# Turning the softmax maps with a diagonal of reciprocals in place of the identity

## What is computed

```python
def attend(q, k, v):                       # layer 0: 16 heads, 4 key/value heads
    s = jnp.einsum("bkgqd,bkld->bkgql", q, k).astype(jnp.float32) * scale
    p = _softmax32(s).astype(v.dtype)
    return jnp.einsum("bkgql,bkld->bkgqd", p, v)
...
def attend(q1, q2, k, v):                  # layer 1: 8 heads, two maps each
    s1 = jnp.einsum("bhqd,bhld->bhql", q1, k[0]).astype(jnp.float32) * scale
    s2 = jnp.einsum("bhqd,bhld->bhql", q2, k[1]).astype(jnp.float32) * scale
    p = _softmax32(s1) - lam * _softmax32(s2)
    return jnp.einsum("bhql,bhle->bhqe", p.astype(v.dtype), v)
```

## Time and profile before

| | |
|---|---|
| median of three runs | 2618.81 us (2612.16, 2618.81, 2623.81) |
| the profiled execution | 2617.47 us, span 2615.7 us, mean granted TensorE clock 0.976 |
| TensorE matmuls, weight loads | busy 94%, 75% |
| VectorE, ScalarE, GpSimd | busy 53%, 43%, 13% |
| costliest group | the dense products of L1510 |
| loop of layer 0 | scores from 147.6 us, last transposes at 238.3 us |
| loop of layer 1 | scores from 865.8 us, last transposes at 954.8 us |
| loop of layer 3 | scores from 2300.9 us, last transposes at 2365.2 us |

### The profile page before, as it was taken

One profiled execution on the slowest core, in us unless ns is written; L12 is line 12 of the kernel. 1 busy time (PEld: TensorE's weight loads), 2 busy tenths in 40 slices (PEclk: granted clock), 3 DMA queues, 4 the chain that ended last, 5 costly groups with the idle time before them and its releaser, 6 DMA issues. The chain is left out here.

```text
span 2615.7 us, 38016 instructions
## 1 busy us (share of the span) xinstructions
PE 2447.6 (94%) x15310; PEld 1966.2 (75%) x15310; DVE 1399.0 (53%) x2162; ACT 1134.9 (43%) x1936; POOL 333.4 (13%) x270
## 2 busy tenths in 40 slices
PE   6989899999999889999999997889999999978997
PEld 3655777778789558777788887777777788947997
DVE  2475565443443766555534335756545435476874
ACT  3365543333342565333323443445333324366663
POOL 0000311111100003111102002322111012002111
PEclk8999999999999999999999998999999999998998
DMA  7611356653232002656532320014656434603663
GB/s 243 212 38 59 112 169 182 185 179 103 78 99 86 25 23 66 186 178 185 175 97 83 104 81 26 2 49 126 187 178 185 136 99 88 160 21 93 183 184 98
DMA packets 500851, 311.32 MB, mean 119 GB/s; under 512 B 24178, under 2 KB 499618, under 8 KB 500548
## 3 DMA queue, kind: packets, MB, share of 16 engines
q1 hardware_dynamic: 498048, 307.39, 39.9%
q10 hardware_dynamic: 2628, 1.50, 0.2%
HBM read 307.80 MB, written 1.05 MB: 118 GB/s over the span
## 5 line engine op out<-in xcount | busy, mean ns | idle before, releaser
L1510 PE MATMUL bank<-h_hi,slab_hi 128*128 128x512 f32 (+1 forms) x2416 | 857.9, 355 | 37.9 <-DVE slab_lo L946 26.0
L1510 PE MATMUL bank<-h_lo,slab_hi 128*128 128x512 f32 (+1 forms) x2416 | 835.8, 346 | 0.0
L1510 PE MATMUL bank<-h_hi,slab_lo 128*128 128x512 f32 (+1 forms) x2416 | 835.3, 346 | 0.0
L946 DVE TENSOR_TENSOR slab_lo<-slab_raw,slab_hi 128x1024 fp32r<-128x1024 f32 (+1 forms) x388 | 538.8, 1390 | 542.6 <-ACT slab_hi L521 541.5
L521 ACT ACTIVATE slab_hi<-slab_raw 128x1024 fp32r<-128x1024 f32 (+1 forms) x388 | 401.5, 1036 | 524.1 <-PE bank L1510 271.2
L1510 PEld LDWEIGHTS bank<-h_hi,slab_hi 128*128 128x128 f32 x2416 | 464.0, 192 | 149.2 <-issue 89.6
L1510 PEld LDWEIGHTS bank<-h_hi,slab_lo 128*128 128x128 f32 x2416 | 464.4, 192 | 55.7
L1510 PEld LDWEIGHTS bank<-h_lo,slab_hi 128*128 128x128 f32 x2416 | 464.5, 192 | 50.0 <-issue 0.5
L915 ACT ACTIVATE conv<-bank,prm 128x512 f32<-128x512 f32 (+1 forms) x176 | 127.3, 723 | 362.7 <-PE bank L1510 362.4
L1510 PE MATMUL bank<-g_hi,slab_hi 128*128 128x512 f32 (+1 forms) x770 | 269.3, 350 | 2.1 <-ACT res_t L572 2.1
L1510 PE MATMUL bank<-g_hi,slab_lo 128*128 128x512 f32 (+1 forms) x770 | 267.2, 347 | 0.0
(11 more groups left out here) (210 smaller groups left out, 2770.1 us busy)
## 6 DMA issues: line engine op xcount, KB each, us to landing
slab_raw<-in_mod_w SPq DMA_DIRECT2D x192, 512.0 KB, 4.6
slab_raw<-in_ffn_w_up SPq DMA_DIRECT2D x176, 512.0 KB, 4.5
slab_raw<-in_ffn_w_down SPq DMA_DIRECT2D x64, 512.0 KB, 4.1
slab_raw<-in_ffn_w_down SPq DMA_DIRECT2D x32, 384.0 KB, 3.6
slab_raw<-in_b_w_qkv SPq DMA_DIRECT2D x24, 512.0 KB, 3.7
slab_raw<-in_c_w_in SPq DMA_DIRECT2D x24, 512.0 KB, 3.7
slab_raw<-in_d_w_qkv SPq DMA_DIRECT2D x24, 512.0 KB, 6.7
slab_raw<-in_a_w_qkv SPq DMA_DIRECT2D x12, 512.0 KB, 5.3
```

What stands on the lines that cost most here:

```text
L946: nc.vector.tensor_tensor(wlo[slot][:, 0:w], raw[of][:, 0:w], whi[slot][:, 0:w].bitcast(f32), ALU.subtract).then_inc(s_lo, 1)
L1510: ins = mm(out, l, r, start=first and n == 0, stop=last and n == 2)
```

## The change

The exponentials stay as they are. The reciprocal of the row sum goes into a diagonal matrix, the identity times the reciprocal as a scalar of each partition, and the block is turned by an ordinary product with this diagonal, which turns and scales at once. In layer 1 the sum of the two maps is formed on the unscaled exponentials: p1 plus p2 times the ratio (second reciprocal times -lambda times the first sum), and the diagonal then holds the first reciprocal. The diagonals have five buffers at the top of the on-chip memory, so the writing of a diagonal waits until the unit five before has been turned. `p_ready` is now raised by the diagonal.

```diff
+        diag_at = [nc.sbuf_usable_end // 64 * 64 - MAPS * 4 * P]
+        diag = [place(f"diag{s}", [P, P], at=diag_at) for s in range(MAPS)]
...
                         for m in range(maps):
                             ins = nc.vector.reciprocal(stat[:, 4 + m, w:w + 1], stat[:, 2 + m, w:w + 1])
                         link(ins)
-                        r1 = stat[:, 4, w:w + 1]
-                        if maps == 1:
-                            nc.vector.tensor_scalar(p1[w % MAPS][:, 0:nk], p1[w % MAPS][:, 0:nk], r1, None,
-                                                    ALU.mult).then_inc(S["p_ready"], 1)
-                        else:
-                            nc.vector.tensor_scalar(p1[w % MAPS][:, 0:nk], p1[w % MAPS][:, 0:nk], r1, None, ALU.mult)
-                            link(nc.vector.tensor_tensor(stat[:, 5, w:w + 1], stat[:, 5, w:w + 1], small[:, 13:14],
-                                                         ALU.mult))
-                            nc.vector.scalar_tensor_tensor(p1[w % MAPS][:, 0:nk], p2[w % MAPS][:, 0:nk],
-                                                           stat[:, 5, w:w + 1], p1[w % MAPS][:, 0:nk],
-                                                           ALU.mult, ALU.add).then_inc(S["p_ready"], 1)
+                        if maps == 2:
+                            ratio = stat[:, 5, w:w + 1]
+                            link(nc.vector.scalar_tensor_tensor(ratio, ratio, small[:, 13:14], stat[:, 2, w:w + 1],
+                                                                ALU.mult, ALU.mult))
+                            nc.vector.scalar_tensor_tensor(p1[w % MAPS][:, 0:nk], p2[w % MAPS][:, 0:nk], ratio,
+                                                           p1[w % MAPS][:, 0:nk], ALU.mult, ALU.add)
+                        if w >= MAPS:
+                            dve.wait_ge(S["p_turned"], w - MAPS + 1)
+                        nc.vector.tensor_scalar(diag[w % MAPS][:], ident, stat[:, 4, w:w + 1], None, ALU.mult).then_inc(S["p_ready"], 1)
...
                         for kt in range(2 if U[w][1] == 0 else 4):
-                            ins = nc.tensor.transpose(pb[:, kt * P:kt * P + P], p1[w % MAPS][:, kt * P:kt * P + P], ident)
+                            ins = mm(pb[:, kt * P:kt * P + P], p1[w % MAPS][:, kt * P:kt * P + P], diag[w % MAPS][:],
+                                     start=True, stop=True)
                         ins.then_inc(S["p_turned"], 1)
```

More of the change, by code:

```diff
@@ L269, in build_program @@
         window = place("window", [P, GRID_W], at=at)
+        assert at[0] <= diag_at[0] - 4 * P * MAPS
         at = [arena + 4 * (16 * T + 4 * D)]
```

## The result

The changed kernel takes 2632.2 us (median of 20 runs, 2626.7 to 2634.4) against 2617.6 for the kernel before in the same comparison: a ratio of 1.0053, 95% interval 1.0046 to 1.0059. By the medians that is 14.6 us, or 0.5%, slower, on the border of what was called measurable. The forecast was 2628.2 with a range of 2614 to 2639: the direction and the range held, and 4 us were missing.

A forecast was written before the change was run, and what follows sets the result against it. Prediction: TensorE becomes the bound in layers 0 and 3, while layer 1 hides its added work. Layer 0 +8.7, layer 1 -1.6 and layer 3 +3.6 give +10.7 on 2617.5, so 2628.2 us; range 2614 to 2639.

The forecast's parts named there:

- The price of a block: Turning on TensorE: an ordinary f32 product takes 0.225 us a block instead of 0.11, +0.115, over 416 blocks.
- an equal price: Turning on TensorE: a product with a diagonal costs what the transpose costs; 2613.6 us; chance 0.12.
- the rival of four transposes: Turning on TensorE: a product costs four transposes, 0.44 against 0.11 us, +0.33 a block; 2693 us; chance 0.02.
- TensorE's sum: Layer 0: TensorE's work in one period without waits, 9.50 us, plus 2.96 added, 12.46, becomes the bound.
- the ring: Layer 0: the period's loop over VectorE and ScalarE, 11.36 us before, grows only by about 0.13.
- The cover: Layer 1: TensorE's 2.49 us idle a period hides its added 1.5 us.
- the rival of a lost cover: Layer 1: if the cover is gone, 1.5 us a period, 10 us; partly gone (+2) within rival (2), chance 0.26.
- the prediction's mixed ring: Layer 3: loop through VectorE and TensorE, one group of transposes +0.53, one scaling -0.20, giving 7.93 us a period.
- the fourth rival: Full clock in layer 3's tail and in 3.4 us at 875 in layer 1: 2627 us; chance 0.10.
- VectorE's 19 us: Narrower scaling saves VectorE 8.6, 4.3 and 6.4 us in layers 0, 1, 3: the most the change could bring.
- rival (1): Product costs what the transpose costs, leaving only VectorE's gain in layers 1 and 3: -3.9, 2613.6 us; chance 0.12.
- Scores apart: Layer 0: two short scores stay apart, +0.64 us a period, +4.5; with layer 1's cover partly gone 2634.7; chance 0.26.

The follow-up runs named there:

- the kernel with the identity product: Kernel before, scaling kept on VectorE, every block turned by an ordinary product with the identity instead of the transpose: 2633.0 against 2619.1 us, ratio 1.0057.
- the partial kernels: Kernel before, identity product only for some layer 0 units: short 2625.1 us, long 2622.8, units 4 and 5 2623.9, units 7, 0 and 1 2622.7.
- the VectorE half: Changed kernel with diagonals written and awaited, but blocks turned by the transpose with the identity, leaving reciprocal scaling out of the result: ratio 0.9998 against the kernel before.
- the kernel with long units alone: Kernel before, identity product instead of the transpose only for layer 0's long units, 16 blocks a period: 2622.8 us, period 11.87 us.
- the filled wait: Kernel before with four never-read 128x128 by 128x512 products put into TensorE's wait ahead of layer 0's loop: 2618.2 us, one run.

## Why the prediction was right or wrong

- **The price of a block: right.** 0.225 us forecast from the earlier trace rows; eight blocks start to start take 1.98 in the changed kernel (208.44 to 210.42 with the step to the next product), 0.25 a block with entering the set included. The rivals of an equal price and of four transposes are out by this pace, and the kernel with the identity product has the same 832 instructions and the same period. (In the rival of four transposes the 5 us for layer 1 are too few: by its own prices 12 x 0.33 + 0.1, less the 2.49 idle, is 1.6 a period and 11 us in all. Nothing hangs on it.)
- **Layer 0's period: right number, half the reason.** 12.46 forecast, 12.50 measured. TensorE's sum was right to 0.04 (12.42 of work by starts), and the kernel with the value products moved shows it at work. The step that failed is the bracket "the ring grows only by about 0.13": the ring passes through three sets of blocks on TensorE, which the first paragraph on layer 0 had itself named as what the score stands behind. Added up from the partial kernels it grows by 0.98 + 0.14 = 1.12, to 12.48, and the wait of 0.08 that is left on TensorE in the changed kernel fits a ring that is just the longer of the two. The two bounds happen to meet, so that the forecast of this period came out is in part luck; had the change touched only the short units, the same reasoning would have said "nothing" for 0.61 a period.
- **Layer 0 in all: +8.7 forecast, +12.1 in the pair of traces.** This is the mis-sized term. Seven periods at +1.10 were charged; there are six regular intervals (+1.14 each, 6.9 us), and the seventh is the tail, which was charged by itself (+0.95 forecast, +0.9 measured). The start was put at nothing, without a reason, and costs 4.4 in this pair of traces: 2.1 for the added passes at full clock, where I can't say for each whom it delays, and the rest for half clock, which stretches eight pairs from 1.09 to 2.00 us. The 6.8 us of half clock stood in the trace of before, at 145.0; the prediction named the clock only in layer 3's tail and at 875 in layer 1.
- **Layer 1: −1.6 forecast, about −0.1 measured** over eleven kernels (above). The cover held: 1.5 us a period of added TensorE work cost nothing (11.93 and 11.94 with the scaling kept), so the rival of a lost cover is out. Failed: seven intervals where there are four regular ones; the ratio kept at 0.153 where it takes 0.220; and the interval behind the regular ones, +0.8 where a tail of +0.3 was counted.
- **Layer 3: +3.6 forecast, +2.1 measured.** The period is near the forecast (7.98, measured 8.05, with 7.96 of work on TensorE), but TensorE's sum alone doesn't hold it: the kernel with the identity product has the same work and 8.11. With the 0.05 that the VectorE half took off in place of 0.20, the prediction's mixed ring would be 7.60 + 0.53 - 0.05 = 8.08 (an estimate), so here too the ring is at least level; no run separates the two in the changed kernel. And there are five regular intervals, not seven (5 x 0.44 = 2.2). The tail was to cost +0.9 with its half clock kept; it is 0.2 shorter, because the half clock of the earlier trace rows is gone. That was the fourth rival's point, and it came true in this place only. Over more traces the layer costs a little more than in this pair: 70.0 to 71.4, mean 70.6, in the seven kernels that leave it as it was, and 72.4 to 73.5, mean 73.1, in the three that hold the whole change in it.
- **VectorE's 19 us: right for layer 0, too high in the others.** "Nothing" in layer 0 held. By rival (1) the VectorE half alone was worth 3.9 us in layers 1 and 3; with the transposes kept it gives a ratio of 0.9998, and 3.9 lies just outside that interval.
- **Scores apart** (second rival): in the changed kernel they go out nearly together, with 0.08 of wait where the rival charged 0.64 a period. Its price, 2634.7, is nearer to the result than the forecast (2.5 us off, against 4.0), but its mechanism is nearly absent. In the kernel with long units alone it does show: four pairs in 1.09 instead of 0.63, a wait of 0.45.
- **Chances.** Slower by over 0.5% had 0.34; the result is 0.53% (0.46 to 0.59), on the line. With the start at its price, and the other layers at what they measured, the sum would have been 10.7 + 3.4 (layer 0) + 1.5 (layer 1) − 1.5 (layer 3) = 14.1, and the chances about even.

The clock in the tail of layer 3, in the kernel before with the filled wait, over the same stretch as the earlier trace rows, where TensorE still does transposes (it stays at 1.00 up to the layer's end):

```profile
2360.25:2363.66 3.41, 1.90 (x16) 1.34 (x18) 2.30 (x7) 2.27 (x7) 0.00 (x0) 1.00 0.00 0
```

So transposes alone don't settle it. Of nine kernels that turn layer 3 by transposes, eight have 3.4 us at half clock between 62 and 64 us into this layer, and this one has not; of five that turn it by products none has. The end from the sixth h_lo on takes 6.2 us with transposes at full clock, 7.4 to 7.7 with half clock, and 7.4 with products at full clock (the two kernels with moved value products left aside): what the product costs in passes it gives back here in clock. By the Trainium skill (TensorE: Matmul & The Clock Gate, Part 4: PE-mode transpose) a transpose doesn't count as activity for the clock as a matmul does; eight of nine against none of five speak for it, and the ninth says that something else weighs in as well.

The Trainium skill's advice to issue a logical transpose as a transpose (Perfetto Trace Analysis, Transposes) agrees with these runs: +14 us for the ordinary product. Its fourfold FP32 speed (TensorE: Matmul & The Clock Gate, Terms) does not: the trace has two pairs of weight load and matmul against one, 2.05 times the time by the starts of the earlier trace rows.

## What to carry to other kernels

Before work is moved from an idle engine to the one that bounds the kernel, follow the ring through the in-order queue: instructions of the full engine that stand ahead of what the others wait for are on the ring, whatever that engine's idle share says, and eight added blocks a period cost 0 or 0.98 us by where they stand. Read a wait on TensorE from starts, not from busy time. Count regular intervals in the trace, and price the start and the tail as pieces of their own, with the clock granted there. The same reading tells what can be moved out of the ring at no cost: 16 value products issued one unit later gave 5 us, where the whole VectorE half of this change gave none.

## What the runs showed of the hardware

- A scalar_tensor_tensor over one column takes 0.220 us with two tensor operands of one column, a tensor_tensor 0.153 to 0.159: even the smallest VectorE instruction has a price by form, and here it cost 0.13 us a period.
- Where the clock falls, and for how long, differs between executions and kernels that are the same up to that point: half clock at layer 0's start lasted 6.8 us in the kernel before and 10.2 in the one with layer 1 alone changed, and the start took 24.1 and 25.4 us. Half a microsecond in a start or tail is therefore nothing to build on from one trace, while the regular periods of a trace repeat to 0.02 us.
- Four products of 128x128 by 128x512 in the wait ahead of the loop kept the clock at 1.00 through its start (with 0.44 us of wait left instead of 4.01), worth 2.9 us of the start in the changed kernel and 0.7 in the one before.
- A set of pairs on TensorE that another kind of product cuts in two takes 0.19 to 0.20 us more (2 x 0.64 for 1.09, 2 x 1.09 for 1.98).
- TensorE's busy time can fill a period and still hide waits, as its ends are modelled: 11.87 of 11.87 with 0.45 of wait by starts.
